# The first modulation computed by halves of the features, with x loaded first and the first products before the second half's loads

## What is computed

```python
def modulation(c, w, b):
    return jnp.split(jax.nn.silu(c) @ w + b, 3, axis=-1)

def sandwich(x, mod, g_pre, g_post, fn):
    shift, scale, gate = mod
    h = rms_norm(x, g_pre) * (1.0 + scale[:, None]) + shift[:, None]
    return x + gate[:, None] * rms_norm(fn(h), g_post)
...
        x = sandwich(x, modulation(c, ada_w[layer, 0], ada_b[layer, 0]), norm_pre[layer, 0], norm_post[layer, 0], mixer)
```

## Time and profile before

| | us |
|---|---|
| median of 3 executions | 1362.15 (1360.89 to 1365.6) |
| the profiled execution, its own time | 1363.03 |
| its span, first to last instruction | 1361.2 |
| PE busy in the span | 1339.1 (98%) |
| DVE busy | 867.1 (64%) |
| ACT busy | 721.4 (53%) |
| mean granted TensorE clock | 0.977 |

### The profile page before, as it was taken

The page is one execution under the profiler, slowest core; times in us unless marked ns, Lnnn a source line. Parts: engine busy times, 40 slices in busy tenths (PEclk is TensorE's granted clock), DMA queues, the critical chain, the costliest instruction groups (busy, mean ns, idle before and its releaser), DMA issues.

```text
span 1361.2 us, 22480 instructions
## 1 busy us (share of the span) xinstructions
PE 1339.1 (98%) x8896; PEld 1211.8 (89%) x8896; DVE 867.1 (64%) x1135; ACT 721.4 (53%) x1070; POOL 50.2 (4%) x76
## 2 busy tenths in 40 slices
PE   9999899999999999999999999999999998999999
PEld 8998699999899779999999899889999896899997
DVE  5688878886799556555565666564455567644554
ACT  3476454444654556444456663655555666655553
POOL 0001000000111000000001000000000000000000
PEclk7899899999999998999999999999999999999999
DMA  9887759996699633555556443455555542355540
GB/s 354 303 322 272 238 198 311 317 309 205 220 328 381 218 78 124 186 187 185 190 179 196 151 160 124 127 183 186 188 188 189 177 165 82 123 193 191 185 155 31
DMA packets 146337, 275.54 MB, mean 202 GB/s; under 512 B 4727, under 2 KB 83343, under 8 KB 146136
## 3 DMA queue, kind: packets, MB, share of 16 engines
q1 hardware_dynamic: 131152, 220.21, 48.0%
q0 software_dynamic: 13872, 52.05, 11.3%
q10 hardware_dynamic: 1240, 2.26, 0.5%
HBM read 273.40 MB, written 1.10 MB: 202 GB/s over the span
## 4 chain that ended last, share of the span: by engine, by line
PE 92%; DVE 4%; ACT 2%; issue 1%; DMA 1%; ACTq 0%; DVEq 0%
PE ps L1962 90%; PE ps L2100 1%; DVE acc_a L1204 1%; DVE wlo L1191 1%; PE ps L2331 1%; DMA ada_ring<-in_ada_w 1%; ACT whi L506 0%; DVE xn L1305 0%; ACT xn L560 0%; PE ps L2439 0%; DVE x L1292 0%; DVE h L1284 0%; DVE x L1299 0%; ACT small L567 0%; DVE hlo L1896 0%
## 5 line engine op out<-in xcount | busy, mean ns | idle before, releaser
L1191 DVE TENSOR_TENSOR wlo<-raw,whi 128x1024 fp32r<-128x1024 f32 x400 | 485.6, 1223 | 363.9 <-ACT whi L506 362.8
L506 ACT CAST whi<-raw 128x1024 fp32r<-128x1024 f32 x400 | 417.7, 1051 | 481.4 <-PE ps L1962 472.8
L1962 PE MATMUL ps<-hhi,whi 128*128 128x256 f32 x1792 | 508.1, 284 | 2.9 <-DVE hlo L1352 2.5
L1962 PE MATMUL ps<-hhi,wlo 128*128 128x256 f32 x1792 | 501.5, 280 | 0.0
L1962 PE MATMUL ps<-hlo,whi 128*128 128x256 f32 x1792 | 501.0, 280 | 0.0
L1962 PEld LDWEIGHTS ps<-hhi,whi 128*128 128x128 f32 x1792 | 337.9, 189 | 9.0 <-issue 6.6
L1962 PEld LDWEIGHTS ps<-hlo,whi 128*128 128x128 f32 x1792 | 338.1, 189 | 4.4 <-issue 2.2
L1962 PEld LDWEIGHTS ps<-hhi,wlo 128*128 128x128 f32 x1792 | 338.2, 189 | 0.0
L1962 PE MATMUL ps<-whi,hidhi 128*128 128x512 f32 x432 | 170.3, 394 | 0.0
L1962 PE MATMUL ps<-wlo,hidhi 128*128 128x512 f32 x432 | 169.1, 391 | 0.0
L1962 PE MATMUL ps<-whi,hidlo 128*128 128x512 f32 x432 | 168.7, 391 | 0.0
(11 more groups left out here) (234 smaller groups left out, 1180.9 us busy)
## 6 DMA issues: line engine op xcount, KB each, us to landing
raw<-in_ffn_w_in SPq DMA_DIRECT2D x44, 1024.0 KB, 6.2
ada_ring<-in_ada_w POOLq DMA_DIRECT2D x40, 1024.0 KB, 7.1
raw<-in_w_mlp_up SPq DMA_DIRECT2D x32, 1024.0 KB, 5.3
raw<-in_w_mlp_down SPq DMA_DIRECT2D x32, 1024.0 KB, 5.0
raw<-in_ffn_w_out SPq DMA_DIRECT2D x22, 1024.0 KB, 5.0
raw<-in_att_w_qkv SPq DMA_DIRECT2D x18, 1024.0 KB, 6.7
raw<-in_w_in_even SPq DMA_DIRECT2D x18, 1024.0 KB, 5.0
raw<-in_hyb_w_in SPq DMA_DIRECT2D x10, 1024.0 KB, 9.7
```

The source lines that it names most:

```text
L506: A.copy(whi[:, H % 4, :], raw[:, slot(n), h * HALF:(h + 1) * HALF]).then_inc(s["hi_ready"], 1)
L1191: V.tensor_tensor(wlo[:, H % 4, :], raw[:, slot(n), h * HALF:(h + 1) * HALF], whi[:, H % 4, :].bitcast(F32), ALU.subtract).then_inc(s["lo_ ...
L1962: return pe.matmul(out, lhsT, rhs, start=first, stop=last, skip_group_check=True)
```

## The change

- **Loads:** x comes first. Then the four loads of shift and scale for features 0 to 511 (a = 0 to 3 now mean that), the upper halves of blocks 0 and 1 of hyb_w_in, the four loads of shift and scale for features 512 to 1023, and the lower halves of the two blocks. `pos` and `vacated` give the slots and their waits.
- **PE's part:** `ada_direct` gives two groups of rows for loads 0 to 3 and 7, and one for 4 to 6.
- **Order on PE:** modulation of the first half, then the products of features 0 to 511 of blocks 0 and 1, the latter between the small products of loads 4 to 7, then the rest of both blocks. `warm_ones` stands at other places with other counts.
- **DVE and ACT** follow the halves: `mod_first(part)` makes shift and scale of four feature groups, `shifted` and `low` are `pre`'s steps on their own, and the norm of x is taken ahead of the bias tables (`vrow`). The gate's first part on DVE (`ada_part`, `acc_a`, block 0) stands between the splits of block 2's first halves.
- Blocks 1 and 2 trade PSUM banks (`pair_of`).

The difference, cut to its core:

```diff
@@ -206,6 +206,8 @@
 
         def pair_of(b):
 
+            if b in (1, 2):
+                return (4, 2)[b - 1]
             if b in (12, 13):
                 return (6, 1)[b - 12]
             if b < 14:
...
+        ADA_POS, HYB_POS = (0, 1, 2, 3, 6, 7, 8, 9), (4, 5, 10, 11)
+
+        def pos(n):
+
+            return HYB_POS[n] if n < 4 else n + ADA_FIRST
+
         def slot(n):
 
-            return (n + ADA_FIRST) % RAW
+            return pos(n) % RAW
 
         def in_count(n):
 
-            return 16 * ((n + ADA_FIRST) // RAW + 1)
+            return 16 * (pos(n) // RAW + 1)
+
...
-            return (3,)
+            return (3,) if a in (4, 5, 6) else (2, 3)
...
+            def vacated(p):
+
+                if p in ADA_POS:
+                    sp.wait_ge(s["ada_used"], ADA_POS.index(p) + 1)
+                    sp.wait_ge(s["ada_pe"], ADA_POS.index(p) + 1)
+                elif p >= 0:
+                    sp.wait_ge(s["lo_ready"], 2 * HYB_POS.index(p) + 2)
+
+            def load_ada(a):
+
+                vacated(ADA_POS[a] - RAW)
+                ap, k = src_cols(t["ada_w"][0, 0], (a // 2 % 2) * 1024 + (a // 4) * 512, a % 2)
+                sp.dma_start(ada_raw(a).rearrange("p (k n) -> p k n", k=k), ap) \
+                    .then_inc(raw_in[ADA_POS[a] % RAW], 16)
+
...
-            for a in range(ADA_FIRST):
-                load(a - ADA_FIRST, 0, src_cols(t["ada_w"][0, 0], (a // 2) * 512, a % 2))
-                if a == 3:
-                    sp.dma_start(x[:, :, :], t["x"][0].rearrange("(t p) n -> p t n", p=P)).then_inc(s["x_in"], 16)
-            proj(FIRST["hyb_in"], t["hyb_w_in"][0], HYB)
+            sp.dma_start(x[:, :, :], t["x"][0].rearrange("(t p) n -> p t n", p=P)).then_inc(s["x_in"], 16)
+            for a in range(4):
+                load_ada(a)
+            for b in range(2):
+                load(b, 0, src_cols(t["hyb_w_in"][0], HYB[b][1], 0))
+            for a in range(4, ADA_FIRST):
+                load_ada(a)
+            for b in range(2):
+                load(2 + b, 0, src_cols(t["hyb_w_in"][0], HYB[b][1], 1))
+            proj(FIRST["hyb_in"] + 4, t["hyb_w_in"][0], HYB[2:])
...
+            norms(0)
+            for tt, lo, hi in ((0, 0, D), (1, 0, 256), (1, 256, D)):
+                act.wait_ge(s["root_x"], tt + 1)
+                act.wait_ge(s["ssq_x"], 2 * tt + 2)
+                A.activation(xn1[:, tt, lo:hi], x[:, tt, lo:hi], ACT.Copy,
+                             scale=small[:, 5, 3 + tt:4 + tt]).then_inc(s["xn_ready"], 1)
+
...
             split(0)
-            pre(0)
+            act.wait_ge(s["mod_ready"], 1)
+            chunk(0, 0)
+            chunk(0, 1)
+            split(1)
+            chunk(0, 2)
+            chunk(0, 3)
+            split(2)
+            split(3)
 
             act.wait_ge(s["lb_step"], 1)
             A.activation(stat[:, 12:16], stat[:, 8:12], ACT.Exp).then_inc(s["lb_act"], 1)
@@ -715,9 +762,21 @@
             act.dma_start(masks[:, :, :], t["masks"]).then_inc(s["band_in"], 16)
             act.dma_start(bandqk[:, :], t["band"]).then_inc(s["band_in"], 16)
             act.dma_start(poolw[:, :, :], t["pool_w"][0].rearrange("g c d -> c g d")).then_inc(s["band_in"], 16)
+            split(4)
+            split(5)
+            act.wait_ge(s["mod_ready"], 2)
+            for i in range(4, KD):
+                chunk(0, i)
+            for H in range(6, 10):
+                split(H)
+            evac(0, 6, *HYB[0][::2], f1, tok1)
+            split(10)
+            split(11)
+            evac(1, 8, *HYB[1][::2], f1, tok1)
             fl = f1[:, :, :].rearrange("p a b -> p (a b)")
-            for b in range(3):
-                proj("hyb_in", HYB[b:b + 1], f1, tok1, b)
+            for b in range(1, 3):
+                if b == 2:
+                    proj("hyb_in", HYB[b:b + 1], f1, tok1, b)
...
+            def mod_first(part):
+
+                c = slice(4 * part, 4 * part + 4)
+                dve.wait_ge(s["cols_sum"], 2 * part + 2)
+                V.tensor_tensor(shcol[:, 0, c], ps[:, 2 + part, 0:4], col("b_shift", 4 * part, 4), ALU.add)
+                link(V.tensor_tensor(scol[:, 0, c], ps[:, 2 + part, 4:8], col("b_scale", 4 * part, 4), ALU.add))
+                V.scalar_tensor_tensor(out=scol[:, 0, c], in0=scol[:, 0, c], scalar=1.0,
+                                       in1=col("g_pre", 4 * part, 4), op0=ALU.add, op1=ALU.mult) \
+                    .then_inc(s["mod_ready"], 1)
+                dve.wait_ge(s["mod_ready"], part + 1)
 
...
+            mean_x(0, 0)
+            mean_x(0, 1)
             for a in range(4):
                 ada_first(a)
-            mean_x(0, 0)
-            mean_x(0, 1)
-            for a in range(4, ADA_FIRST):
-                ada_first(a)
-            mod_cols(0, 0)
+            mod_first(0)
+            shifted(0, 1)
             split(0)
-            pre(0)
+            low(0, 0)
+            low(0, 1)
+            shifted(0, 3)
+            split(1)
+            low(0, 2)
+            low(0, 3)
+            split(2)
+            ada_first(4)
+            ada_first(5)
+            split(3)
+            ada_first(6)
+            ada_first(7)
+            split(4)
+            mod_first(1)
+            shifted(0, 5)
+            low(0, 4)
+            low(0, 5)
+            shifted(0, 7)
+            split(5)
+            low(0, 6)
+            low(0, 7)
+            split(6)
+            split(7)
...
-            proj("hyb_in", HYB[0:1], 0)
-            ada_block(acc_a, 0, 0)
-            proj("hyb_in", HYB[1:2], 1)
+            ada_part(acc_a, 0, 0, 0)
+            split(8)
+            split(9)
+            ada_part(acc_a, 0, 0, 1)
+            split(10)
+            split(11)
...
                 for i in range(4 * nb, 4 * nb + 4):
-                    m = mm(ps[:, 0, i:i + 1], acc_a[:, i * P:(i + 1) * P], ones[:, 0:1], False, True)
+                    c = i % 8
+                    m = mm(ps[:, 2 + nb // 2, c:c + 1], acc_a[:, i * P:(i + 1) * P], ones[:, 0:1], False, True)
                 m.then_inc(s["cols_sum"], 1)
 
             def warm_ones(n):
@@ -2170,41 +2268,59 @@
                 for _ in range(n):
                     mm(ps[:, 1, 0:P], ones[:, :], ones[:, :])
 
+            def warm_cols(n):
+
+                for _ in range(n):
+                    mm(ps[:, 2, 2 * P:3 * P], ones[:, :], ones[:, :])
+
             def ada_cols(a):
 
-                pe.wait_ge(raw_in[a % RAW], 16 * (a // RAW + 1))
-                for kk in ada_direct(a):
+                ada_raw_in(pe, a)
+                rows = ada_direct(a)
+                for kk in rows:
                     k = 4 * (a % 2) + kk
                     for i in range(4):
-                        c = 4 * (a // 2) + i
-                        m = mm(ps[:, 0, c:c + 1], raw[:, a % RAW, kk * 512 + i * P:kk * 512 + (i + 1) * P],
-                               sc[:, k:k + 1], a == 0 and i == 0, False)
+                        c = 4 * (a // 2 % 2) + i
+                        m = mm(ps[:, 2 + a // 4, c:c + 1], ada_raw(a)[:, kk * 512 + i * P:kk * 512 + (i + 1) * P],
+                               sc[:, k:k + 1], a % 4 == 0 and kk == rows[0] and i == 0, False)
                 m.then_inc(s["ada_pe"], 1)
 
             pe.wait_ge(s["one_ready"], 1)
             warm_ones(24)
             pe.wait_ge(s["sil_c"], 1)
-            ada_cols(0)
-            warm_ones(8)
             pe.wait_ge(s["const_in"], 48)
             for g in range(DG):
                 mm(ps[0:8, 4 + g, 0:VLEN_DIL], vtab[:, 8 * g:8 * g + 8], voh[:, g * VLEN_DIL:(g + 1) * VLEN_DIL]) \
                     .then_inc(s["vec_dil"], 1)
             mm(ps[0:8, 7, :], vtab[:, 24:32], voh[:, 3 * VLEN_DIL:]).then_inc(s["vec_dil"], 1)
-            for a in range(1, ADA_FIRST):
-                ada_cols(a)
-                warm_ones(2)
-                if a in (3, 5):
-                    add_cols(a // 2 - 1)
-                if a == 5:
-                    pe.wait_ge(s["vec_dil_c"], 4)
-                    turn(0)
-                if a == 6:
-                    add_cols(2)
+            ada_cols(0)
+            warm_ones(8)
+            ada_cols(1)
+            pe.wait_ge(s["vec_dil_c"], 4)
+            turn(0)
+            ada_cols(2)
+            add_cols(0)
+            warm_ones(4)
+            ada_cols(3)
+            warm_ones(4)
+            add_cols(1)
+            warm_ones(8)
+            for h in range(2):
+                proj_half(HYB[0][0], pair_of(0), h, h, 0, 0)
+            ada_cols(4)
+            proj_half(HYB[1][0], pair_of(1), 2, 0)
+            ada_cols(5)
+            add_cols(2)
+            proj_half(HYB[1][0], pair_of(1), 3, 1)
+            ada_cols(6)
+            ada_cols(7)
+            warm_cols(4)
             add_cols(3)
-            warm_ones(12)
-
-            proj("hyb_in", HYB[0:2], j=0)
+            warm_cols(8)
+            for h in range(2, 4):
+                proj_half(HYB[0][0], pair_of(0), h + 2, h, 0, 0)
```

(39 more changed lines are left out.)

53 lines of the change are left out of this document (21 added, 32 removed).

## The result

The changed kernel takes 1375.69 us (median of 4, 1373.19 to 1377.67) against 1363.1 for the kernel before on the same chip: ratio 1.0086, 95% interval 1.0062 to 1.011, slower. Two of the 24 executions of the kernel before in that second set were far slower than the rest (1631 and 3353 us) and are left out of the ratio. The loss is some 7 to 13 us.

What follows compares the result with a forecast made beforehand. PE, busy at half clock with small products, was taken as the bound. Blocks 0 and 1 end at 62.4 + 1.5 + 11.3 = 75.2 against 68.25, 7.0 us later: 1362.15 + 7.0 = 1369.2, range 1364 to 1376.

Steps and rivals of the forecast that it cites:

- the likeliest case: Whole kernel: first product at 39 to 44, the middle's clock fall or none, +4.5 to +10.5 us, 1366.5 to 1372.5.
- the wider one: Whole kernel: the range with three of the rivals added to the forecast, 1364 to 1376.
- The bound: Ahead of the projection: PE's small products at half clock, 0.213 us per pass, set the first product, not the loads.
- x first: Start of the loads: each load moves back some 2.7 us, hidden by PE's small products, so costed at nothing.
- PE ahead of the first product: From the start: 144 passes, mostly at half clock, after bias tables begun at 9.0; first product at 41.3.
- First half of block 0 and the middle: Behind the first product: 5.6 us plus 0.5 for clock, 80 passes 9.4, block 1's half 5.65: 62.4; clock fall adds 1.5.
- Blocks 0 and 1 done: End of both blocks on PE: 62.4 + 1.5 + 11.3 = 75.2 against 68.25, 7.0 us later.
- The gate's block on DVE: DVE behind the halves: `acc_a` block 1 some 3.5 us later, covered by a 4.03 us wait: nothing, other end 3 us.
- rival D: Gate's ring: `acc_a` block 1, its successor's load and block 3's splits late, PE behind: 3 us more, 1372.2; chance 0.10.
- Rival C: PE's later wait of 3.36 us at 151.5 takes up to 3.4 us of the shift: 1365.8; chance 0.08.
- Rival B: Ahead of the first product: eight dummies bring the clock back a while, 3.4 us of the loss go: 1365.8; chance 0.13.
- Rival A: First half on PE: clock stays at 2.4 GHz, first product at 28.5, time 1354.4; chance 0.11.

Runs made afterwards that it cites:

- e7: The kernel before with only the larger share for PE (two groups of rows of loads 0 to 3 and 7): 1372.36 us, ratio 1.0064.
- e1: The kernel before without the two dummies behind the small products of each of loads 1 to 7: 1361.01 us, ratio 0.9978.
- e4: The changed kernel without the dummies behind loads 0, 2 and 3 (8 + 4 + 4): ratio 1.002 to the kernel before.
- e8: The kernel before with x loaded first and nothing else changed: median 1366.51 us, ratio 1.0018.
- e12: e6 with x loaded behind load 3, as before the change: ratio 1.0014 to the kernel before.
- e9: The changed kernel again, unaltered, as a second set of executions: 1371.43 us against 1364.41 for the kernel before, ratio 1.0058.
- e2: The changed kernel with one group of rows per load on PE, as before the change: 1362.66 us, ratio 0.9978 to the kernel before.
- e3: The changed kernel with the gate's first block on DVE in one piece ahead of block 2's splits: ratio 1.0048 to the kernel before.
- e6: The changed kernel with one row group per load on PE, gate's block in one piece, no dummies behind loads 0, 2, 3: 1356.89 us, ratio 0.9943.
- e5: The changed kernel with one group of rows per load on PE and the gate's first block in one piece: 1358.29 us, ratio 0.9969.
- e10: e6 with none of the modulation's rows on PE, DVE multiplying all four groups: ratio 0.9958 to the kernel before.

## Why the prediction came out as it did

The median, 1375.69, lies above the likeliest case's range (1366.5 to 1372.5) and at the very edge of the wider one (1364 to 1376).

The bound was right. PE at half clock, not the loads, sets the start: in front PE is busy without a gap while DVE waits 18.34 us for it, and a pass costs what the earlier trace rows say. e7, with more passes on PE, moved the first product by 6.05 of the 7.7 us summed; in e1 and e4 the start moved by about the sum, but with other changes of clock and waits in it. The loads are not far: in e1 PE waits for two of them.

**x first, priced at nothing: wrong by itself, since work of PE must lie in front.** e8 costs 2.5 us in the old order, because PE runs out of dummies before load 0 comes. In the changed kernel the bias tables stand in that place, so a gap of 0.9 us ahead of load 0 remains (11.35 to 12.29 on PE's weight loads, part of it the last table's product). The tables in turn wait for their own load (`voh`): they began at 9.4 to 9.9 in all ten profiles of the new order, where I had taken 9.0, and in eight of them PE stood idle for it, 0.9 to 1.24 us. And e12 shows that there x first is what the halves need.

**PE ahead of the first product:** 41.3 forecast, 41.76 measured, 44.18 in e9.

**First half of block 0 and the middle:** 62.4 forecast for the end of the middle at full clock. The last dummies ran from 61.32, and the first product behind them came at 64.67, 2.3 us after the forecast. Of these, 1.2 were there at 48.61 (47.4 forecast): 0.5 from the later first product, and most of the rest because the first 2.6 us of products ran at half clock, some 1.3 us lost where I had put 0.5. Then the clock fell at some 61.4, and the last 16 dummy passes took 3.35 us, not 1.87. I had put a fall at 3.1 us with one chance in two, so 1.5. It came in both profiles of this kernel and in e2, e3 and e4, and it cost 1.6 us here and 3.1 in e9. That the 1.5 fits this profile is luck: the chance was too low and the price, here, too high.

**Blocks 0 and 1 done:** 75.2 forecast, 76.08 measured.

**The gate's block on DVE, priced at nothing with 3 us as the other end: this is the term that failed.** I compared DVE's lateness with its wait for ACT, 4.03 us, and left out what hangs on it one step further. The ring's next load starts only when DVE has used the one before. It started at 82.71 (73.80 before, which is 1.1 more than the shift of 7.8) and took 12.15 us to its use (10.7 before). That it was slower because it followed the bias and gain rows (`gg`, `grow`) more closely, 3.2 us behind the last of them instead of 6.3, is my reading and not tested by itself. DVE's multiplication `bandqk` came late, PE waited 1.09 us for it, and up to the attention products 2.2 us were lost, 1.3 of them at `bandqk` and the rest in small steps that I did not trace. This is rival D, for which I gave 3 us and a chance of 0.10, but with PE waiting for `bandqk` and not for the splits of block 3. e3, which undoes only this, has the distance at 55.37.

**Rival C** did not come: the later waits of PE kept their length (3.36 us at 162.5 for 3.36 at 151.5). **Rival B** is real, but as a matter of the single execution (seen in e3, whose program on PE is the same), and is worth about twice what I had put. This kernel's times spread over 9 us (1368.95 to 1378.28), and the slowest have the lowest mean clocks, 0.974 to 0.977; that it is this stretch which makes them differ is likely, not shown. **Rival A** never came in a profile of this kernel.

I forecast 7.0 us more than before. The first set of executions gave 12.6 more, the second 7.0. In the profiled execution of the first (12.1 more), the 5.1 that I lacked are 0.8 up to the end of block 1, 2.2 by the ring, and 2.2 behind the transposes of the next layer, of which the clock between 510 and 545 is some 1.7. The second set's agreement is partly luck, since its profile shows the ring's loss too (distance 56.90) and a dearer fall in the middle. How often each clock pattern comes stays open: it would take many profiles of one kernel.

By its parts, each read from single edits so that they need not add up, the change is this: halves with x first, a gain of some 5 us (e6 against e1, which have as many small products and dummies: 0.9943 against 0.9978, intervals just apart); the larger share for PE, a loss of 9 to 15 us (e7, e2); more dummies in a queue of work, a loss of 5 to 9 us beside the larger share (e4), and nothing clear beside the smaller (e5, e6); the gate's block in pieces, 1 to 2 us in the profiles (e5, e3), too little for the ratios to show.

## What to carry to other kernels

PE, 100% busy at half clock, was the bound here however small its instructions were, and work given to it cost its price at that clock: count the passes that stand ahead of the first real product. An idle neighbour (DVE here, 18.3 us) is where such work belongs, up to the point where it becomes tight itself (e10). Dummies are nearly free only where the engine would wait; and behind any reordering follow the ring loads that its consumers release, one step further than the first cover.

## What the runs showed of the hardware

- Busy time alone did not bring the clock back. In the changed kernel PE was busy without a gap from 14 to 44 us at 0.50, with products of one column, and dummies and transposes between them. The Trainium skill (TensorE: Matmul & The Clock Gate, "Part 4: PE-mode transpose") says that transposes do not bring about the full clock. Some traces agree: it stayed at 0.50 through the 16 transposes at 21.38 here, as at 29.33 before. Others do not: with no dummies since the start's or load 0's, it came back at 30.5 in e1, within the transposes that began at 27.75, at 24.5 in e4, behind those from 20.39 to 23.84, and at 18.5 in e10, behind those from 14.59. So the measurement does not bear the rule out for every execution; what tells them apart no run here shows. A clock that is up already is used by transposes: 16 in 1.82 us in e3, against 3.46.
- The same program comes out differently from one execution to the next, by whether a run of 16 dummy passes brought the clock back (e3: at 1.00 from 18 to 24; the changed kernel: not). That moved the first product by 6.3 us, more than most of the edits did.
- A 1 MB load of the gate's ring took 12.15 us from its start to its use with other loads, of its own queue and of SP's, under way; in the kernel before, the 40 such loads took 5.5 to 11.3 us, 7.1 in the median.
